# Expert choice beside the end of the mixer: seven tiles' affinities copied ahead of the eighth, the prompt tiles' residual added on TensorE, their eviction and last root on ScalarE

## What is computed

```
x1     = x + mix @ w_out                      # mix: conv part and gated mLSTM heads
tokens = rms_norm(x1, norm2_g)                # x1 * rsqrt(mean(x1*x1) + eps) * g
aff    = softmax(tokens @ w_router, axis=-1)  # 16 affinities a token
gate, idx = top_k(aff.T, cap)                 # cap = 32 (prompt), 128 (sample) tokens an expert
ye     = (silu(xe @ w_gate) * (xe @ w_up)) @ w_down * gate      # xe = tokens[idx]
out    = x1 + scatter_add(ye, idx);  y = rms_norm(out, final_g)
```

## Time and profile before

| | us |
|---|---|
| median of 3 runs (1325.57 to 1327.87) | 1325.58 |
| time of the profiled execution | 1325.75 |
| its span, first to last instruction | 1324.0 |
| PE busy in the span | 1268.0 (96%) |
| DVE busy | 905.9 (68%) |
| ACT busy | 737.6 (56%) |
| POOL (GpSimd) busy | 326.4 (25%) |

### The profile page before, as it was taken

How to read it: one execution, slowest core, us unless ns; L and a number is a source line. 1 busy time by engine, 2 the same in 40 slices (tenths; PEclk the granted TensorE clock), 3 DMA queues, 4 the chain that set the end, 5 groups by cost and what they waited for, 6 DMA issues and landing times.

```text
span 1324.0 us, 25237 instructions
## 1 busy us (share of the span) xinstructions
PE 1268.0 (96%) x9868; PEld 1041.6 (79%) x9868; DVE 905.9 (68%) x1302; ACT 737.6 (56%) x1064; POOL 326.4 (25%) x317
## 2 busy tenths in 40 slices
PE   7999999999999999949999999999999999999993
PEld 6669997666677888749888988898889888988892
DVE  5354122431485566798888888888898889888975
ACT  8356322113335544336677667766676667666763
POOL 3322221010052222121332223222323231323040
PEclk8999999999998999969999999999999999999997
DMA  8122454351268774279899999999999999999995
GB/s 281 48 72 83 127 179 151 104 147 32 80 211 245 208 207 148 81 235 338 275 316 319 336 304 311 320 336 306 305 317 338 309 303 316 337 312 303 299 364 206
DMA packets 242031, 314.76 MB, mean 238 GB/s; under 512 B 16096, under 2 KB 206048, under 8 KB 241968
## 3 DMA queue, kind: packets, MB, share of 16 engines
q1 hardware_dynamic: 226576, 268.54, 61.4%
q0 software_dynamic: 15392, 45.36, 11.6%
HBM read 274.41 MB, written 39.44 MB: 237 GB/s over the span
## 4 chain that ended last, share of the span: by engine, by line
PE 90%; DVE 4%; ACT 3%; DMA 1%; issue 1%; SPq 0%; POOL 0%; DVEq 0%; ACTq 0%; POOLq 0%
PE psum L2142 23%; PE psum L2020 16%; PE psum L2149 11%; PE psum L1998 9%; PE psum L2165 8%; PE psum L1890 8%; PE psum L2183 4%; PE psum L2174 4%; PE psum L1945 1%; PE psum L2135 1%; ACT yt L1187 1%; PE psum L1909 1%; PE psum L1950 1%; PE psum L1871 1%; DMA woraw<-in_w_out_dram 1%
## 5 line engine op out<-in xcount | busy, mean ns | idle before, releaser
L1738 DVE TENSOR_TENSOR elo<-eraw,ehi 128x2048 bf16<-128x2048 f32 x192 | 433.1, 2282 | 1.0 <-POOLq L809 1.0
L1157 ACT ACTIVATE ehi<-eraw 128x2048 fp32r<-128x2048 f32 x192 | 362.2, 1902 | 27.3 <-PE psum L2183 18.6
L2142 PE MATMUL psum<-xc,ehi 128*128 128x320 f32 x2048 | 331.9, 314 | 2.1 <-DVE xc L1743 2.1
L2142 PEld LDWEIGHTS psum<-xc,ehi 128*128 128x128 f32 x2048 | 303.8, 189 | 3.6 <-DVE xc L1743 2.4
L2149 PE MATMUL psum<-xb,elo 128*128 128x160 bf16 x2048 | 163.9, 233 | 0.0
L1751 DVE TENSOR_REDUCE gu<-psum 128x320 f32<-128x640 f32 x128 | 105.0, 820 | 83.8 <-PE psum L2149 83.6
L2149 PEld LDWEIGHTS psum<-xb,elo 128*128 128x128 bf16 x2048 | 138.5, 98 | 13.1
L2020 PE MATMUL psum<-hn_nar,wnar 128*128 128x512 bf16 (+1 forms) x768 | 145.0, 346 | 2.7 <-DVE wnar L1304 2.7
L2165 PE MATMUL psum<-ehi,hc 128*128 128x512 f32 x512 | 132.6, 406 | 0.0
L2020 PEld LDWEIGHTS psum<-hn_nar,wnar 128*128 128x128 bf16 x768 | 73.6, 99 | 66.7 <-issue 4.5
L2165 PEld LDWEIGHTS psum<-ehi,hc 128*128 128x128 f32 x512 | 95.1, 188 | 22.2
(11 more groups left out here) (275 smaller groups left out, 1668.2 us busy)
## 6 DMA issues: line engine op xcount, KB each, us to landing
eraw<-in_w_gate_dram SPq DMA_DIRECT2D x64, 1024.0 KB, 7.6
eraw<-in_w_up_dram SPq DMA_DIRECT2D x64, 1024.0 KB, 8.6
eraw<-in_w_down_dram SPq DMA_DIRECT2D x64, 1024.0 KB, 14.1
wraw<-in_w_in_dram SPq DMA_DIRECT2D x12, 1024.0 KB, 7.9
negm<-negm_d SPq DMA_DIRECT2D x10, 512.0 KB, 6.8
acc_d<-x POOLq DMA_DIRECT2D x10, 512.0 KB, 5.5
tok_d<-tk POOLq DMA_DIRECT2D x10, 512.0 KB, 3.2
v<-v_d SPq DMA_DIRECT2D x18, 256.0 KB, 3.9
```

The source lines that it names most:

```text
L1157: act.activation(f["ehi"][:, j % RING, :], f["eraw"][:, raw_slot(s, j), :], ACT.Copy).then_inc(S["ehi"], 1)
L1738: dve.tensor_tensor(f["elo"][:, j % RING, :], f["eraw"][:, raw_slot(s, j), :], f["ehi"][:, j % RING, :].bitcast(F32), ALU.subtract).then_i ...
L2142: pe.matmul(o[:, 0:2 * NC], hi[:, k, c], x[:, k, :, :].rearrange("p a t -> p (a t)"), start=(k == 0), stop=False, skip_group_check=True)
```

## The change

Line numbers in the pieces below are those of each kernel; `L1100` is the new `residual_out`, `L1919` the new product with the identity, `L1973` the affinities' transposes, `L1148` and `L1717` the sample's `AFF` copies, `L1113` and `L1170` the one-element activations that change the table.

1. TensorE adds the residual of the two prompt tiles. Ahead of the first block of `project` for tiles 8 and 9 a product of `xs` with the identity (float32, 512 columns, four in all) opens the PSUM bank. ScalarE evicts the bank (`residual_out`), VectorE no longer does.
2. The affinities of tiles 0 to 6 are transposed and copied by ScalarE (512 and 384 columns) as soon as tile 6 has them. The eighth tile's are transposed behind the first block of `project(8, 1)`, and VectorE copies those 128 columns itself.
3. The last root of the prompt tiles is a ScalarE `Sqrt` (with a change of the activation table to Sqrt before and back to Exp behind it) and four VectorE instructions (`polish`) in place of twelve.
4. ScalarE copies the prompt's affinities into `AFF`, in place of VectorE.
5. The rounds stand in other places: 2 in step 9, 3 in step 10, 5 + 1 in step 11, and one behind the loop ahead of the last four. In the string at line 2114 there are 48 transposes in place of 56.

```diff
@@ scalar stream
+            def residual_out(m, h):
+                act.wait_ge(S["o_ps"], 2 * m + h + 1)
+                if h == 0:
+                    act.wait_ge(x1_out[m % 2], 16 * (m // 2))
...
+                act.activation(d["x1"][:, m % 2, 512 * h:512 * h + 512], psum[:, 6 + h, :], ACT.Copy
+                               ).then_inc(S["x1_done"], 1)
             for n in range(NT + 2):
+                if n >= NT:
+                    columns_out(n - 2, 1)
                 if n == NT + 1:
-                    columns_out(n - 2, 1)
+                    act.activation(spare_col, b["eps1"][:, 0:1], ACT.Sqrt)
...
+                if n == NT - 1:
+                    act.wait_ge(S["choiceT_ps"], NS - 1)
+                    for i, w in ((0, half_width), (1, half_width - P)):
+                        act.activation(AFF[HALF2 * i:HALF2 * i + NE, 0:w], psum[0:NE, (0, 4)[i], 0:w], ACT.Copy
+                                       ).then_inc(S["aff_out"], 1)
                 if n >= 2 and not joint(n - 2):
                     softmax_terms(n - 2)
+                if n == NT - 1:
+                    residual_out(n - 1, 0)
...
+                if n == NT:
+                    residual_out(n - 1, 0)
                 if 1 <= n <= NT:
                     columns_out(n - 1, 0)
-                if n == NT - 1:
-                    act.wait_ge(S["choiceT_ps"], 1)
-                    for i in range(NS // 4):
-                        act.activation(AFF[HALF2 * i:HALF2 * i + NE, :], psum[0:NE, (0, 4)[i], :], ACT.Copy
-                                       ).then_inc(S["aff_out"], 1)
                 if n < NT:
                     heads_high(n)
                 if n == NT - 1:
+                    residual_out(n - 1, 1)
                     scaled_tokens(LATE)
+                if n == NT:
+                    residual_out(n - 1, 1)
+            act.wait_ge(S["sum2"], NT)
+            act.activation(d["ms"][:, :, 1, H:H + 1], d["ms"][:, :, 0, H:H + 1], ACT.Sqrt, bias=b["eps1"][:, 0:1]
+                           ).then_inc(S["rooted"], 1)
+            act.activation(spare_col, b["eps1"][:, 0:1], ACT.Exp)
             for m in range(NS, NT):
                 softmax_terms(m)
             for m in range(NS, NT):
                 scaled_tokens(m)
+            act.wait_ge(S["choiceT_ps"], NS + 1)
+            act.activation(AFF[PROMPT:SEL, 0:SP_], psum[0:NE, 1, 0:SP_], ACT.Copy).then_inc(S["aff_out"], 1)
@@ vector stream
             def last_roots():
                 dve.wait_ge(S["sum2"], NT)
-                inverse_root(d["ms"][:, :, 1, H:H + 1], d["ms"][:, :, 0, H:H + 1], d["ms"][:, :, 2, H:H + 1])
+                ch(dve.tensor_scalar(d["ms"][:, :, 2, 0:1], d["ms"][:, :, 0, H:H + 1], EPS, None, ALU.add))
+                dve.wait_ge(S["rooted"], len(BATCHES) + 1)
+                polish(d["ms"][:, :, 1, H:H + 1], d["ms"][:, :, 2, 0:1], d["ms"][:, :, 2, H:H + 1])
...
                 if n == NT:
-                    choose(both_halves, half, CAPS, 1, 4)
+                    choose(both_halves, half, CAPS, 2, 5)
+                    logit_peak(m)
...
-                if 1 <= n <= NT:
+                if 1 <= n <= NS:
                     residual(n - 1, 0)
...
                     dve.wait_ge(S["aff_out"], NS // 4)
-                    choose(both_halves, half, CAPS, 0, 1)
-                if n == NT:
-                    logit_peak(m)
-                    choose(both_halves, half, CAPS, 4, 6)
+                    dve.wait_ge(S["choiceT_ps"], NS)
+                    last = slice(half - P, half)
+                    ch(dve.tensor_copy(AFF[HALF2:HALF2 + NE, last], psum[0:NE, 4, last]))
+                    choose(both_halves, half, CAPS, 0, 2)
...
                 if n == NT + 1:
-                    choose(both_halves, half, CAPS, 6, 7)
+                    choose(both_halves, half, CAPS, 5, ROUNDS_BEFORE)
                     last_roots()
...
-                    choose(both_halves, half, CAPS, 7, 8)
+                    choose(both_halves, half, CAPS, ROUNDS_BEFORE, ROUNDS_BEFORE + 1)
...
-            choose(both_halves, half, CAPS, 8, 12)
-            dve.wait_ge(S["choiceT_ps"], 2)
-            ch(dve.tensor_copy(AFF[PROMPT:SEL, 0:SP_], psum[0:NE, 1, 0:SP_]))
+            choose(both_halves, half, CAPS, ROUNDS_BEFORE + 1, 12)
+            dve.wait_ge(S["aff_out"], NS // 4 + 1)
             choose(slice(0, SEL), half, CAPS, 12, CAPS // 8)
@@ tensor stream
                 c = slice(512 * h, 512 * h + 512)
+                if k0 == 0 and joint(n):
+                    pe.wait_ge(ld_x[n % 2], 16 * (n // 2 + 1))
+                    pe.matmul(psum[:, 6 + h, :], ident[:, :], d["xs"][:, n % 2, c], start=True, stop=False)
...
+                if n == NT - 1:
+                    pe.wait_ge(S["aff_done"], NS - 1)
+                    pe.wait_ge(S["ht_done"], NT)
+                    for i in range(NS - 1):
+                        transpose_affinities(i).then_inc(S["choiceT_ps"], 1)
                 if 2 <= n <= NT:
                     project(n - 1, 0, 4, KD)
-                    project(n - 1, 1, 0, 4)
+                    project(n - 1, 1, 0, 1)
+                if n == NT - 1:
+                    pe.wait_ge(S["aff_done"], NS)
+                    pe.wait_ge(S["aff_out"], NS // 4)
+                    transpose_affinities(NS - 1).then_inc(S["choiceT_ps"], 1)
                 if 2 <= n <= NT:
+                    project(n - 1, 1, 1, 4)
                     transpose_rows(n - 1, 0)
...
-            for _ in range(56):
+            for _ in range(48):
                 pe.transpose(psum[:, 2, 0:P], ident[:, :], ident[:, :])
```

More of the change, by code:

```diff
@@ L1093, in _ @@
             for n in range(NT + 2):
+                if n >= NT:
+                    columns_out(n - 2, 1)
                 if n == NT + 1:
[L1095 removed]
+                    act.activation(spare_col, b["eps1"][:, 0:1], ACT.Sqrt)
                 if n >= 2:
                     token_squares(n - 2)
[L1098 to L1101 removed]
+                if 2 <= n < NT:
+                    columns_out(n - 2, 1)
+                if n >= NT:
+                    logit_parts(n - 2)
                 if n < NT:
@@ L1890, in project @@
                         mm = pe.matmul(psum[:, 6 + h, :], x, w,
-                                       start=(k == 0 and a == 0), stop=(k == KD - 1 and a == 2))
+                                       start=(k == 0 and a == 0 and not joint(n)), stop=(k == KD - 1 and a == 2))
                 if k1 == KD:
@@ L1931, in logits, with transpose_affinities @@
                 pe.matmul(psum[:, logit_bank(m), 0:NE], quarter_sums, expert_sum, start=True, stop=True).then_inc(S["lg_ps"], 1)
+            def transpose_affinities(i):
+                return pe.transpose(psum[0:NE, (0, 4)[i // 4], (i % 4) * P:(i % 4 + 1) * P], aff[:, i, :], ident[:, :])
             def numerators(n):
```

27 lines of the change are left out of this document (13 added, 14 removed).

## The result

| | before | changed |
|---|---|---|
| median, us | 1325.34 (16 runs, 1322.98 to 1327.87) | 1328.55 (16 runs, 1323.39 to 1330.65) |
| profiled execution, and its span | 1325.75, 1324.0 | 1329.14, 1327.4 |
| mean granted TensorE clock | 0.978 | 0.979 |

The ratio of the changed kernel to the one before is 1.0023, with a 95% interval of 1.0015 to 1.0031: **3.0 us slower** (2.0 to 4.1). Forecast were 3.65 us faster, 1321.9, in a range of 1319.5 to 1325.0. The time is outside it, on the other side.

What follows compares the result with a forecast made beforehand. VectorE's selection chain up to the last index was taken to hold the start of the experts. Gains of 0.7, 1.35, 1.15 and 0.45 sum to 3.65 us, giving 1321.9 us, range 1319.5 to 1325.0.

Steps and rivals of the forecast that it cites:

- Queues: GpSimd's token products, stores and weight loads 5 and 6 come 3.7 us later, overlapping the gather some 1.2; costed at nothing.
- Sum: Adds 0.7, 1.35, 1.15 and 0.45 to a 3.65 us gain, round 13 at 574.15 against 577.81.
- product with the identity: Each of four float32 512-column TensorE products in the output projection takes 0.89 us, scaled from a 129-column row.
- first round: VectorE's first selection round begins at 541.0, 1.65 us earlier, after its own copy of the eighth tile's affinities.
- wait for the heads' high part: Behind round 2 VectorE newly waits 1.5 us for ScalarE's mxh before the heads' low part.
- wait for the squares: Ahead of the last root VectorE waits 0.9 us more, for ScalarE's squares behind the Sqrt table load.
- last root: The prompt tiles' root on ScalarE plus four VectorE instructions takes 1.25 us in place of 2.38, gaining 1.15.
- B: Rival: VectorE's waits don't come, its own work alone sets the end; gain 6.25 us, 1319.3; chance 0.15.
- C: Rival: the first gather collides with two weight loads and lands 3.9 us later; gain 0.75, 1324.8; chance 0.14.
- D: Rival: each activation table change costs about twice its row, 1.4 us more before the squares; 1323.3; chance 0.10.
- E: Rival: TensorE's clock falls at the projection's end, squares 14.8 us later, a loss of 11, 1333; chance 0.04.
- F: Rival: eighth tile's transpose or a copy is late by an unseen queue, start stays at 542.6; 1325; chance 0.07.

Runs made afterwards that it cites:

- a_dm_waits_cut: Changed kernel with GpSimd's drain moved to its idle time, third selection round ahead of the heads' low part, Sqrt table loaded before tile 9's last eviction; 1320.16 us, ratio 0.9975.
- a_nodrain: Changed kernel with GpSimd's drain at the barrier replaced by a bare semaphore increment; measured 1.9 us faster than the kernel before (0.4 to 3.3).
- a_drain_moved: Changed kernel with GpSimd's drain moved from the barrier to its idle time ahead of the last x1 store; median 1323.04 us, 1.6 faster than before.

## Why the prediction was wrong

**The step that failed is "Queues".** Its ground is laid in the first part, "After 562.26 nothing else holds the experts back": true before by 1.2 us only. "Queues" followed GpSimd's token products, "3.7 later", to the stores and the weight loads 5 and 6 behind them, asked whether these would collide with the gather, and costed all of it "at nothing". It did not ask what GpSimd itself does behind its stores. It goes to the barrier for which TensorE's index transpose waits, and its drain takes 9.06 us. The number was to be had: the drain stood in the trace of before, ended 1.2 us ahead of the transpose, and 3.7 us of lateness less 1.2 of cover makes the transpose 2.5 later than before in place of 3.65 sooner. Measured: 2.28. What hides this in the trace of before is the release in the transpose's row, "DVE GIF": it names the last to come and doesn't say that a second one came a microsecond ahead of it.

**"Sum"** inherited this: it took round 13 for the end. With the drain the end hangs on the prompt's affinities, and for these the change is a loss. The three rounds that it puts ahead of the last root cost VectorE's own path nothing, since they are only moved, and 6.84 us on the way to the affinities, of which the shorter root and the rest of the change give back half.

The steps on VectorE held in the trace, with the 0.73 taken off:

| step | forecast | measured |
|---|---|---|
| product with the identity | 0.89 | 0.85 |
| first round | 541.0 | 540.94 |
| wait for the heads' high part | 1.5 | 1.50 |
| third round | 547.7 | 547.59 |
| wait for the squares | 0.9 | 0.84 |
| last root, 2.38 before | 1.23 left | 1.13 |
| last root to round 13, the prompt affinities' copy | 0.45 | 0.49 |
| round 13, gain | 3.65 | 3.92 |

Its parts being right, the gain of VectorE was not right by luck in the trace; how much of it reaches the time stays open, as said below. The price of the product stands in TensorE's rows, as the way from its start to that of the second product behind it, less the 0.23 of the first:

```profile
539.43 1.02 PE L1919 MATMUL psum<-xs,ident 128*128 128x512 f32 x2
539.88 0.79 PE L1928 MATMUL psum<-woh,mxh 128*128 128x512 f32 x1
540.51 0.39 PE L1928 MATMUL psum<-wol,mxh 128*128 128x512 f32 x1
```

**The rivals.** None describes what happened. B (the waits don't come) is refuted by both waits; taking out one of them in a_dm_waits_cut was worth 1.5 at T. C (the gather collides) is refuted by a_nodrain: the quarter-row gather runs beside loads 5 and 6 (DMA share 1.06 in 588 to 592), lands in 4.1 us, against 3.9 in the kernel before, and the gathered rows' transposes start with no idle behind the 48. The 588.4 of "Queues" for the gather was misread: it is issued at 590.39 before, so at 586.7 by the forecast. D (a table load of twice its row): the load starts at 565.00 and the squares at 566.41, 1.41 in all, dummy included, where the forecast has 1.40:

```profile
565.00 1.28 ACT L1113 ACT_TABLE_LOAD   x1
566.30 0.20 ACT L1113 ACTIVATE router<-eps 128x1 f32<-128x1 f32 x1
566.41 1.04 ACT L1072 ACTIVATE junk<-x 128x1024 f32<-128x1024 f32 x1
```

By the rule of the Trainium skill ("ScalarE: Activation LUTs", What ACT_TABLE_LOAD costs), 2.66, an estimate for the squares' start is 567.7; the trace disagrees here too. E (the clock falls in the projection): the granted clock stayed 1.00 in every window from 544 to 563 us. Its sum was wrong as well: squares 14.8 later, less 3.65, is a loss of 11 against before, and so 1336.7, not 1333. F was for a late queue, but at the eighth tile's transpose, and that one came in time. The side "slower" had 0.05, all of it for reasons that did not come.

**What stays open.** In two kernels the median gained less than the trace says, by more than its interval: a_drain_moved by 2.0 us, a_dm_waits_cut by 1.8. The profiles show scatter of that size behind T: from T to the first expert's output it took 54.6 to 57.6 us, by whether the clock was at its low level in the 48 transposes and in expert 0's first products (these took about 4.1 us in most profiles; in a_drain_moved's they took 2.58, and the clock stayed at 1.00 through 588 to 612). This stretch is 56.4 in before's profile. In a_dm_waits_cut's it is 57.2, which makes 4.3 of the 5.1 and brings it into the interval; in a_drain_moved's it is 55.2, so that its profile, 1320.5 us, is the fastest of its executions (median 1323.0). One profile a kernel can't tell whether the earlier start makes the low clock more frequent. The signs don't hang on it; how much of VectorE's 3.9 us comes through does.

## What to carry to other kernels

Where an engine meets others at a barrier, price every engine's way to it, not only the one whose release the row names: look for who came second and by how much, since that is all the cover there is. If work is moved ahead of a value that another engine needs, cost it on that engine's path too; here 3.4 us of lateness at GpSimd, with 1.2 of cover, made a loss of 2.3 out of 3.9 gained on VectorE. And where GpSimd has issued many transfers, a drain early in its idle time takes the nine microseconds off the barrier, for 0.2 to 0.3 at the end of the program, or for 0.30 at the barrier if the second drain is kept. Whether a kernel may do without the drain behind its last stores has to be settled for each; nothing here shows it in general.

## What was not expected of the hardware

- GpSimd's drain took about 0.04 us and 0.082 for each transfer that it had issued since its last one (worked out from five lengths), whatever their size, at the barrier though their landing had been waited for: 9.06 us for 110, 1.03 for 12, 0.30 for three.
- Leaving the drain out makes the end of the program 2.2 to 2.3 us longer (11.43 for 9.25 and 11.46 for 9.15 behind the last scatter's issue); with an early one alone it is 9.44 to 9.49, with an early and a late one 9.25, as with one at the barrier (9.15 to 9.25).
- Two changes of the activation table and a root on ScalarE beat twelve small VectorE instructions by 0.46 us, and four 512-column evictions on VectorE beat four float32 products with the identity and their waits by 0.2, both by T in one profile each.
